# Turning the second four feature blocks between the products of the first four, at the beginnings of stages

## What is computed

```python
# first stack, layer l: modulate, mixer, layer norm, modulate, feed-forward, layer norm
x = layer_norm(ALPHA * x + gate2 * mixer(modulate(x, shift0, scale1)), g0, b0)
x = layer_norm(ALPHA * x + gate5 * conv_ffn(modulate(x, shift3, scale4)), g1, b1)
# second stack, layer l
proj = rms_norm(x, attn_norm) @ w_in
x = x + concat(o_mla, o_diff, o_chunk) @ w_out
x = x + conv_ffn_2(rms_norm(x, ffn_norm))
```

## Time and profile before

| | us |
|---|---|
| median of 3 runs (1653.02 to 1653.48) | 1653.36 |
| the profiled execution | 1651.02 |
| its span (first to last instruction) | 1649.70 |
| TensorE busy | 1593.9 (97%) |
| VectorE busy | 1045.8 (63%) |
| ScalarE busy | 803.6 (49%) |
| GpSimd busy | 238.1 (14%) |
| mean granted clock of TensorE | 0.995 |

### The profile page before, as it was taken

One profiled execution on the slowest core, in us unless ns is written; L12 is line 12 of the kernel. 1 busy time (PEld: TensorE's weight loads), 2 busy tenths in 40 slices (PEclk: granted clock), 3 DMA queues, 4 the chain that ended last, 5 costly groups with the idle time before them and its releaser, 6 DMA issues.

```text
span 1649.7 us, 26875 instructions
## 1 busy us (share of the span) xinstructions
PE 1593.9 (97%) x10838; PEld 1379.2 (84%) x10838; DVE 1045.8 (63%) x1936; ACT 803.6 (49%) x1517; POOL 238.1 (14%) x284
## 2 busy tenths in 40 slices
PE   6999999999999999999999999999999999999998
PEld 4778778877777888787899988878999888799986
DVE  3553866465354534688787767666777657767765
ACT  2332974333133323468465553655555546655553
POOL 1110430011010100012011101142111012321110
PEclk9999999999999999999999999999999999999999
DMA  9557022353564324021345553424455533345552
GB/s 378 217 226 276 13 85 103 126 232 122 210 256 179 102 81 149 27 77 53 153 180 205 179 190 122 142 90 167 159 188 187 198 132 128 114 145 186 187 200 77
DMA packets 39418, 257.27 MB, mean 156 GB/s; under 512 B 5504, under 2 KB 6784, under 8 KB 10496
## 3 DMA queue, kind: packets, MB, share of 16 engines
q1 hardware_dynamic: 36416, 249.61, 41.3%
q0 software_dynamic: 1296, 4.72, 0.8%
q10 hardware_dynamic: 1584, 1.23, 0.3%
HBM read 254.49 MB, written 1.05 MB: 155 GB/s over the span
## 4 chain that ended last, share of the span: by engine, by line
PE 82%; DVE 9%; ACT 4%; DMA 2%; issue 1%; POOL 0%; SPq 0%; DVEq 0%; ACTq 0%
PE ps L485 25%; PE ps L487 24%; PE ps L486 24%; PE ps L501 2%; PE ps L632 1%; PE ps L654 1%; PE ps L641 1%; DVE wl L1761 1%; DVE ps L2020 1%; DMA arena<-in_xT 1%; PE ps L527 1%; ACT wh L1319 1%; PE ps L1070 1%; ACT arena L1667 1%; DMA raw<-in_ev_w_in 1%
## 5 line engine op out<-in xcount | busy, mean ns | idle before, releaser
L1761 DVE TENSOR_TENSOR wl<-raw,wh 128x1024 fp32r<-128x1024 f32 (+2 forms) x324 | 378.3, 1209 | 373.2 <-ACT wh L1319 372.7
L1319 ACT CAST wh<-raw 128x1024 fp32r<-128x1024 f32 (+2 forms) x334 | 328.8, 1034 | 510.1 <-PE ps L487 395.9
L485 PE MATMUL ps<-xh,wh 128*128 128x256 f32 (+1 forms) x1582 | 493.8, 312 | 2.3 <-issue 2.1
L487 PE MATMUL ps<-xh,wl 128*128 128x256 f32 (+1 forms) x1582 | 488.9, 309 | 0.0
L486 PE MATMUL ps<-xl,wh 128*128 128x256 f32 (+1 forms) x1582 | 488.9, 309 | 0.0
L485 PEld LDWEIGHTS ps<-xh,wh 128*128 128x128 f32 x1582 | 302.0, 191 | 27.2 <-issue 11.6
L486 PEld LDWEIGHTS ps<-xl,wh 128*128 128x128 f32 x1582 | 302.1, 191 | 15.1 <-issue 0.7
L487 PEld LDWEIGHTS ps<-xh,wl 128*128 128x128 f32 x1582 | 302.0, 191 | 15.2
L485 PE MATMUL ps<-wh,xh 128*128 128x512 f32 (+3 forms) x812 | 299.1, 368 | 13.5 <-DVE xl L2152 6.5
L487 PE MATMUL ps<-wh,xl 128*128 128x512 f32 (+3 forms) x812 | 294.5, 363 | 0.0
L486 PE MATMUL ps<-wl,xh 128*128 128x512 f32 (+3 forms) x812 | 294.5, 363 | 0.0
(11 more groups left out here) (212 smaller groups left out, 1822.5 us busy)
## 6 DMA issues: line engine op xcount, KB each, us to landing
raw<-in_ada SPq DMA_DIRECT2D x48, 1024.0 KB, 7.5
raw<-in_up SPq DMA_DIRECT2D x44, 1024.0 KB, 5.6
raw<-in_fin SPq DMA_DIRECT2D x44, 1024.0 KB, 4.8
raw<-in_down SPq DMA_DIRECT2D x22, 1024.0 KB, 4.8
raw<-in_fout SPq DMA_DIRECT2D x22, 1024.0 KB, 4.9
raw<-in_win SPq DMA_DIRECT2D x12, 1024.0 KB, 4.9
raw<-in_ev_w_in SPq DMA_DIRECT2D x9, 1024.0 KB, 8.0
raw<-in_wout SPq DMA_DIRECT2D x8, 1024.0 KB, 4.8
```

Source lines behind the costliest of these rows:

```text
L485: e.matmul(out, A[0], B[0], start=first, stop=False)
L487: return e.matmul(out, A[1], B[0], start=False, stop=last)
L1319: e.copy(hi_of(j)[:, a:b], raw_of(j)[:, a:b]).then_inc(*S.hi.up((j, half)))
L1761: e.tensor_tensor(lo_of(j)[:, a:b], raw_of(j)[:, a:b], hi_of(j)[:, a:b].bitcast(F), ALU.subtract).then_inc(*S.lo.up((j, half)))
```

## The change

`features` becomes a generator, `turning`, that stops after each block; a new `features(turns, n)` draws n blocks from it. The products' loops take such a generator and draw one block after the products of each k. Where eight blocks were turned ahead of the products, four are now turned ahead and the others follow behind P0, P1, P2 and P3; for `("f1", 1)`, with its two banks, two are turned ahead and the other six follow behind P0 to P5. `("f", 0, 1)` still turns four at a time. Nothing else is changed: the same instructions, on TensorE in another order; the programs of the other engines are the same.

```diff
-        def features(key, tiles, ks, banks, wait):
+        def turning(key, tiles, ks, banks, wait):
...
                     free[b] = [(S.act if by_act(key, k) else S.vec, ("feat", key, k))]
+                yield
+
+        def features(turns, n=8):
+
+            for _ in range(n):
+                next(turns, None)
+            return turns
...
-        def tokens(name, i, key, tiles, xkey=None, turns=True):
+        def tokens(name, i, key, tiles, xkey=None, turns=True, turn=iter(())):
...
                     wait_feature(xkey, k)
                     for t in tiles:
                         product(t, k)
+                    next(turn, None)
...
-        def by_features(up, key, g):
+        def by_features(up, key, g, turn=iter(())):
...
                 for part in range(2):
                     m = hidden(up, 0, part, g, 256, [k])
+                next(turn, None)
...
-        mixed("ev", "ev_w_out", 2, (0, 2), lambda: turn_tiles(("f", 0, 0), 0, 0, (0, 1), range(4), [6, 7, 2, 3]))
-
-        turn_tiles(("f", 0, 0), 0, 0, (0, 1), range(4, 8), [6, 7, 2, 3])
-        by_features("up0", ("f", 0, 0), 0)
+        turn = turn_tiles(("f", 0, 0), 0, 0, (0, 1), range(8), [6, 7, 2, 3])
+        mixed("ev", "ev_w_out", 2, (0, 2), lambda: features(turn, 4))
+
+        by_features("up0", ("f", 0, 0), 0, turn)
...
-        down_rows("down0", 2, lambda: turn_tiles(("f1", 0), 0, 1, (0, 1), range(4), [6, 7, 2, 3]))
-
-
-        turn_tiles(("f1", 0), 0, 1, (0, 1), range(4, 8), [6, 7, 2, 3])
+        turn = turn_tiles(("f1", 0), 0, 1, (0, 1), range(8), [6, 7, 2, 3])
+        down_rows("down0", 2, lambda: features(turn, 4))
...
-        od_keys(t2, ("f1", 0))
+        od_keys(t2, ("f1", 0), turn)
         od_queries(0)
-        turn_tiles(("f1", 1), 0, 1, (2, 3), range(8), [6, 7])
-        od_keys((2, 3), ("f1", 1))
+        od_keys((2, 3), ("f1", 1), features(turn_tiles(("f1", 1), 0, 1, (2, 3), range(8), [6, 7]), 2))
...
-        turn_tiles(("f", 1, 0), 1, 0, t2, range(8), [4, 5, 6, 7])
-        first_hidden("up1", ("f", 1, 0))
+        first_hidden("up1", ("f", 1, 0), features(turn_tiles(("f", 1, 0), 1, 0, t2, range(8), [4, 5, 6, 7]), 4))
...
-            rms_tiles(("a", l), ("x1", 1) if l == 0 else ("f", 0))
+            turn = features(rms_tiles(("a", l), ("x1", 1) if l == 0 else ("f", 0)), 4)
...
                         if k == 3:
                             m.then_inc(*S.proj.up((key, t), ("use", j)))
+                    next(turn, None)
...
-            rms_tiles(("b", l), ("a", l))
-            first_hidden(f"fin{l}", ("b", l))
+            first_hidden(f"fin{l}", ("b", l), features(rms_tiles(("b", l), ("a", l)), 4))
```

More of the change, by code:

```diff
@@ L758, in ffn, with first_hidden @@
                     ada_finish(FINISH_AT[f])
-        def first_hidden(up, key):
-            by_features(up, key, 0).then_inc(*S.proj.up((up, 0, 0), (up, 0, 1), ("use", J[up, 0])))
+        def first_hidden(up, key, turn):
+            by_features(up, key, 0, turn).then_inc(*S.proj.up((up, 0, 0), (up, 0, 1), ("use", J[up, 0])))
             hidden_free(up, 0)
@@ L855, in turn_tiles @@
             last = 4 if l == 0 else 2
-            features(key, tiles, ks, banks, lambda k: [
+            return turning(key, tiles, ks, banks, lambda k: [
                 (S.vec, ("xh", l, which, t, k // 4)) if t == last - 1 else (S.act, ("xh", l, which, t)) for t in tiles])
-        mixed("ev", "ev_w_out", 2, (0, 2), lambda: turn_tiles(("f", 0, 0), 0, 0, (0, 1), range(4), [6, 7, 2, 3]))
-        turn_tiles(("f", 0, 0), 0, 0, (0, 1), range(4, 8), [6, 7, 2, 3])
-        by_features("up0", ("f", 0, 0), 0)
+        turn = turn_tiles(("f", 0, 0), 0, 0, (0, 1), range(8), [6, 7, 2, 3])
+        mixed("ev", "ev_w_out", 2, (0, 2), lambda: features(turn, 4))
+        by_features("up0", ("f", 0, 0), 0, turn)
         wait_chunk(J["up0", 1])
@@ L866, in tensor_program @@
             hidden("up0", 1, part, 0, 256)
-            turn_tiles(("f", 0, 1), 0, 0, (2, 3), range(4 * part, 4 * part + 4), [6, 7, 4, 5])
+            features(turn_tiles(("f", 0, 1), 0, 0, (2, 3), range(4 * part, 4 * part + 4), [6, 7, 4, 5]), 4)
         by_features("up0", ("f", 0, 1), 1).then_inc(*S.proj.up(("up0", 0, 0), ("up0", 0, 1), ("use", J["up0", 0])))
@@ L873, in tensor_program, with od_keys @@
         ffn("up0", "down0", 2, 2, True, gates((0, 5), 2, [6]))
-        down_rows("down0", 2, lambda: turn_tiles(("f1", 0), 0, 1, (0, 1), range(4), [6, 7, 2, 3]))
-        turn_tiles(("f1", 0), 0, 1, (0, 1), range(4, 8), [6, 7, 2, 3])
-        def od_keys(tiles, xkey):
-            bs = tokens("od_w_in", 4, "okv", tiles, xkey, turns=False)
+        turn = turn_tiles(("f1", 0), 0, 1, (0, 1), range(8), [6, 7, 2, 3])
+        down_rows("down0", 2, lambda: features(turn, 4))
+        def od_keys(tiles, xkey, turn):
+            bs = tokens("od_w_in", 4, "okv", tiles, xkey, turns=False, turn=turn)
             for t in tiles:
@@ L929, in rms_tiles @@
         def rms_tiles(key, at):
-            features(key, t2, range(8), [4, 5, 6, 7], lambda k: [
+            return turning(key, t2, range(8), [4, 5, 6, 7], lambda k: [
                 (S.vec, ("xr", *at, 0)), (S.act if k >= 4 else S.vec, ("xr", *at, 1, k // 4))])
```

## The result

| | before | after |
|---|---|---|
| median of the timed runs, us | 1653.15 (5 runs) | 1660.51 (5 runs, 1658.70 to 1662.04) |
| the profiled execution, us | 1651.02 | 1660.40 |
| its span, us | 1649.70 | 1659.1 |
| mean granted clock of TensorE | 0.995 | 0.991 |

The ratio is 1.0045, with a 95% interval from 1.0034 to 1.0056. The changed kernel was measured once more among the experiments, on another chip and against the kernel before on that chip: 1.0038 (1.0028 to 1.0048). Forecast was 1657.9 with a range of 1652.0 to 1662.0.

A forecast was written before the change was run, and what follows sets the result against it. TensorE was taken as the bound nearly everywhere (82% of the span). Gains of 0.98, 0.90 and 0.75 us (-2.6) and a loss of 7.2 at layer 1's keys gave +4.6: 1657.9 us, range 1652.0 to 1662.0.

The forecast's parts named there:

- the rival with a second fall of the clock: Keys' second half: clock also at the lower level inside the staircase, +4 us on top, 1662; chance 0.09.
- Second stack's feed-forward parts: Starts of both parts: products start earlier, four blocks' transposes lie inside the stream; gain 0.49 us each, -0.98 together.
- Its projections: Starts of both second-stack projections: 0.50 us gained, a new wait of about 0.2 mostly paid back; 0.45 each, -0.90.
- Layer 1's feed-forward part: Its start: first products can run at 808.74 instead of 810.36; gain 1.62 - 0.87 = 0.75 us.
- The starts with four tiles: Two starts normalising four tiles at once: products still wait 1.09 us for VectorE's low part; gain 0 at both.
- The keys' second half: Layer 1, two banks: overlap becomes a staircase of 3.20 us steps, features 6.0 late, queries late; +5.75 without a clock fall.
- The clock: TensorE at keys and queries: no fall in the staircase, one after the 4.0 us idle, costing 1.54; shift becomes 7.2.
- slower still: Keys' second half: lower clock inside the staircase as well, +4 us on top, 1662; chance 0.09.
- The rival without any fall: Keys and queries: staircase but no fall of the clock, +5.75 - 2.6 = +3.1 us, 1656.5; chance 0.25.
- faster: Keys' second half: overlap works, products follow one another, queries' weights ready in time; -6.0 us, 1647.3; chance 0.10.
- the rival that the weights aren't late: Queries after the keys: ScalarE and VectorE catch up, only TensorE's own 1.6 us stays; -1.0, 1652.3; chance 0.14.

The follow-up runs named there:

- keys alone: Only the second half of layer 1's keys changed against the kernel before (two blocks ahead, eight everywhere else): 1662.88 us, ratio 1.0055.
- keys as before, weights early: Changed kernel, but all eight blocks turned ahead at the keys' second half and the queries' weights converted ahead of those features: 1649.60 us, ratio 0.9978.
- the fillers: Changed kernel with unused matmuls in TensorE's gaps at the keys (3, then 2 in each later gap, 8 ahead of the queries): 1657.33 us, ratio 1.0022.
- twelve fillers: First group in an earlier run: changed kernel with 12 unused matmuls ahead of the keys' first products, 6 to 28 in later gaps: 1676.65 us, ratio 1.0140.
- keys as before: Changed kernel, but the second half of layer 1's keys turns all eight blocks ahead: 1650.18 us, ratio 0.9985.
- before with the weights early: Kernel before, with the queries' weights converted ahead of the features of the keys' second half: 1652.92 us, ratio 0.9998.

## Why the prediction was right

The direction and the place were right, and the measured 1660.51 lies in the range; the point of 1657.9 was 2.6 too low. The range held because its top had been set by the rival with a second fall of the clock. Step by step:

1. **Second stack's feed-forward parts** (0.49 each): 0.45. Right; TensorE's first product stands 0.52 behind the first low part, as forecast.
2. **Its projections** (0.45 each): 0.30. The wait for the low weights appeared, but it was dearer than forecast. Listed as 0.18, it put the column 0.34 behind its place: its first product starts at 1032.99, while the last product before it starts at 1032.46 and these products are 0.19 apart, so 1032.65 was its turn. I had charged 0.2. The interleaving itself gave 0.42 and not 0.50, and 0.22 was paid back at the next column, where the 0.24 of before is gone: 0.42 - 0.34 + 0.22 = 0.30.
3. **Layer 1's feed-forward part** (0.75): 0.71.
4. **The starts with four tiles** (0): P6 waits as long as before, 1.13 for 1.09.
5. **The keys' second half.** The pattern was forecast in its detail: steps of 3.20 (3.15), TensorE idle 4.0 before the queries (4.01), the queries 5.64 late (5.78 where the clock held), released by the weights' low part on VectorE. The cause that I named, the order of scale and low part in VectorE's loop, is only one of two that give the same step; with the other order the depth of two gives 2.85 to 3.13.
6. **The clock**, the term that was mis-sized. I charged one fall at 1.54, the loss of the earlier trace rows, and placed it at the queries. It comes there in every profile with the 4 us wait and no fillers, and costs 2.2 in both profiles of the changed kernel, 1.55 to 2.6 in the others. And in the first profile and, in part, in the run with the keys alone, another fall came inside the staircase, for 4.19 in the first. That is the rival "slower still", which had it at 4. I expected none because products stand between the transposes, and the runs show that this is no protection: this stretch had products in every step and the clock fell all the same, in one execution and not in another. The Trainium skill ("TensorE: Matmul & The Clock Gate", "Part 4: PE-mode transpose") says that transposes don't count as TensorE activity for its clock. I had read it as support for that step, and it does not settle the matter: the trace of the kernel before agrees with it, but in the profile of keys as before, weights early, the same eight blocks were turned by themselves and the clock stayed at 1.00.

The sum for the changed kernel's second profile, +8.03 - 2.2 = +5.8, and for the first, +12.2 - 2.2 = +10, against the forecast +4.6. The second profile as a whole is 7.0 longer than the one of before, as its keys begin 1.2 later (693.98 for 692.75). The timed runs, +7.4 and +6.3 by the two ratios, lie between. How often the fall inside the staircase comes is not shown; two profiles of the changed kernel have it once. The rival without any fall (+3.1) is what the fillers made of it: +3.6. The rival "faster" fell with the staircase, and the rival that the weights aren't late fell with the 4.01.

## What to carry to other kernels

Before turning (or loading, or converting) fewer blocks ahead, compare the depth with the latency of a block through the other engines: here, with 2.06 us of pipeline against 0.72 of products, two made a staircase and four did not. By these numbers three might do (an estimate, not run). Then read what stands behind these blocks in each consumer's queue, for a step that becomes late drags its successors along; moving the weights' conversion ahead of the features was worth nothing before the change and 5 to 7 us after it. And charge a new idle stretch of TensorE with a fall of its clock beside the wait itself: here 1.5 to 2.6 us behind a wait of 3.6 to 4.0 us.

## What was not expected of the hardware

- The same program with the same gaps of 1.06 us in TensorE's stream had its clock at 0.50 in one execution (700 to 705) and at 1.00 in another. A profile of one execution can't price such a term; the timed runs can.
- A wait of 3.6 to 4.0 us ahead of dense products was followed by the lower clock in all five profiles that had it and no fillers: 5.76 us of products took 7.3 to 8.4.
- A filler matmul on plain float32 operands is two matmul instructions: twelve fillers of 256 columns are 24 in the trace, 5.35 us in all, 0.22 each. A transpose of float32 is one: two blocks of two tiles are the x4 in the first rows of the keys.
- Eight blocks turned by themselves were followed by the lower clock in three profiles (before, keys as before, and before with the weights early) and not in a fourth (keys as before, weights early).
